# A dense SwiGLU stage with seven-product tiles: lag of the low parts, token sums on another engine, four plain tiles, parts of 5, 5, 6 and 6

## The chip, the cores and the metric

The program runs on one core of a Trainium2 chip. The metric is the device time of one execution in microseconds. Engines are PE (TensorE), DVE (VectorE), ACT (ScalarE), POOL (GpSimd) and SP (SyncE, which here issues most of the loads).

## What is computed

Two layers of a hybrid backbone act on 640 tokens (128 context tokens and 512 latent tokens) of width 1024. The change touches one stage, the dense channel mixer of layer 0, with D_FF = 2816:

```python
def swiglu(u, w_gate, w_up, w_down):
    return (jax.nn.silu(u @ w_gate) * (u @ w_up)) @ w_down
...
    h = rms_norm(x, g_pre2) * (1 + scale2) + shift2
    x = x + gate2 * rms_norm(ffn(h), g_post2)
```

## The kernel before, in words

**Operands in two parts.** Every float32 operand of a product is kept as a high part (a rounded copy in fp32r, made by ACT) and a low part (the rest, made by DVE as operand minus high part). One product is three matmuls: high by high, high by low, low by high. `block_high` (L2766) and `block_low` (L2769) convert a weight block of 128 x 512; `high` (L2757) and `low` (L2761) convert a whole piece of 128 x 1024.

**Tiles.** `stage_dense` walks over 22 feature tiles f of 128 columns of D_FF. The first `PLAIN_F` tiles are plain: gate and up are one piece each, and `features` (L3039) issues 8 k-blocks x 3 x 2 token halves = 48 matmuls of 320 columns per piece, 96 for a tile. The other tiles are combined tiles: a Strassen-like scheme computes gate and up together with seven products (`PRODUCTS`: gate_top, t1, t2, gate_bottom, t3, up_bottom, t4), each 4 x 3 = 12 matmuls of 320 columns (`product`, L3051), 84 for a tile. The four weights t1 to t4 are differences of raw weight blocks (`combine`, L3157, on DVE), each of which is then split like any other block. t1 is up_top minus gate_top, t2 is up_bottom minus t1, t3 is up_bottom minus up_top, t4 is gate_bottom minus t2; t1 and t2 overwrite gate_top's raw block, so each can be formed only when the one before it has been read. The scheme also wants token sums s1 to s4 of the four quarters of the activations (128 x 1280 each), formed once at the stage's start: s1, s2 and s4 on POOL (7 operations, L2881 to L2889), s3 on DVE (3 operations, L3248 to L3250).

**What follows a product.** ACT copies three partial results out of PSUM (`keep_p1` L2925 after gate_top, `keep_p5` L2931 after t1, `keep_u2` L2936 after t2). DVE adds three more to them (`mix_gate` L3203 after gate_bottom, `mix_second` L3209 after t3, `mix_first` L3215 after up_bottom). ACT applies Silu (L2942, and L2947 after t4), DVE multiplies (L3221), ACT takes the high part of the hidden tile (`hidden_high`, L2952), DVE the low part (`hidden_low`, L3227). PE waits for keep_p1 before t2, for keep_u2 before t3, and for mix_gate and mix_second before t4.

**Order.** All queues are written out by hand. On each engine a loop over the entries e (an entry is a weight block in the order in which PE uses it) does what follows the product just finished, and then `make(e + 6)`: ACT the high part and DVE the low part of the block six entries on. The ring holds 8 blocks, so ACT may convert a block when PE has finished the entry seven back. DVE's make waits for ACT's high part of the same block; it also forms the next difference:

```python
                dve.wait_ge(w.hi_done, e + 1)
                w.block_low(dve, e)
                if kind == "gate_top":
                    dve.wait_ge(*w.arrival(entry_of("up_bottom", f)))
                    dve.wait_ge(w.lo_done, e + 1)
                    combine(f, "t1")
```

**Parts.** The tiles come in `DENSE_PARTS`. After each part but the last, PE multiplies the part's hidden tiles by w_down in two column halves (L3089; per tile 2 x 5 token blocks x 3 matmuls of 512 columns = 30), and DVE adds the sums to an accumulator (`keep_sums`, L3237 and L3239). In the last part (L3127) token block b is the outer loop, with 6 matmuls per tile and block, so 30 per tile as well. After block b its residual chain runs on DVE and ACT: add L3292, gate L3297, square and root L3002 and L3004, residual L3306, norm L467, L469, L486 and L494, and PE turns the block (`norm.turn`, L504, 8 small matmuls) after the matmuls of block b + 1. The gate rows that L3297 needs come by a DMA (`ex_rows`) that ACT issues near the end. The next stage begins with L593.

**Loads.** SP loads the raw pieces into four rooms. A room is loaded again when the low part of its last reader is done.

Of the kernel before, what the change touches and what calls it, by code (L numbers as in the profile page):

```python
# [13 lines left out]
F32 = mybir.dt.float32  # L14
# [2627 lines left out]
DENSE_PARTS = (6, 6, 6, 4)  # L2642
DENSE_DEEP = max(DENSE_PARTS)
PLAIN_F = 3
# [6 lines left out]
class DenseWeights:  # L2651
# [10 lines left out]
    RAW_AT = 22816  # L2662
    HI_AT = 28960
    HL_AT = HI_AT + 4 * RING * BLOCK
    LO_AT = HL_AT + 4 * DENSE_DEEP * T + 128
# [5 lines left out]
    def __init__(self, p, l, side, at):  # L2671
# [4 lines left out]
        self.wl = p.placed(f"ex_w_lo{l}", [P, self.RING, BLOCK], F32R, at + self.LO_AT)  # L2676
        sem = lambda name: p.ctx.enter_context(p.nc.semaphore(f"{name}{l}"))
# [54 lines left out]
    def raw_of(self, f, name):  # L2732

        gate, up = self.raw(self.piece_of["gate", f, None]), self.raw(self.piece_of["up", f, None])
        top, bottom = slice(0, BLOCK), slice(BLOCK, 2 * BLOCK)
        return {"gate_top": gate[:, top], "t1": gate[:, top], "t2": gate[:, top], "gate_bottom": gate[:, bottom],
                "t3": up[:, top], "up_bottom": up[:, bottom], "t4": gate[:, bottom], "up_top": up[:, top]}[name]

# [26 lines left out]
    def block_high(self, act, e):  # L2765
        act.activation(self.wh[:, e % self.RING], self.source(e), ACT.Copy).then_inc(self.hi_done, 1)  # L2766

    def block_low(self, dve, e):
        dve.tensor_tensor(self.wl[:, e % self.RING], self.source(e), self.wh[:, e % self.RING].bitcast(F32),  # L2769
                          ALU.subtract).then_inc(self.lo_done, 1)  # L2770


def stage_dense(p, l, h, acc, side, w, at, following, last):
# [12 lines left out]
    token_sum, token_difference, token_high, token_low, pool_c = (p.sig(f"dense_{n}") for n in (  # L2786
        "token_sum", "token_difference", "token_high", "token_low", "pool_chain"))
# [9 lines left out]
    rows = p.placed(f"ex_rows{l}", [P, 2 * D], F32, at + w.S1_AT)  # L2797
    gates = rows[:].rearrange("p (q k s) -> p s k q", k=KD, s=2)
    junk_room = p.placed(f"ex_junk{l}", [P, D], F32, at + w.S2_AT)
# [63 lines left out]
    with nc.Block() as block:  # L2863
# [11 lines left out]
        @block.gpsimd  # L2875
        def _(pool):
            link = chained(pool_c)
            pool.wait_ge(*before.low.at(1))
            plain = lambda half: half.bitcast(F32)
            s1, s2, s4 = s1_raw[:], s2_raw[:], s4_raw[:]  # L2880
            link(pool, pool.tensor_tensor(s1, plain(a21[0]), plain(a22[0]), ALU.add))  # L2881
            link(pool, pool.tensor_tensor(s1, s1, plain(a21[1]), ALU.add))
            pool.tensor_tensor(s1, s1, plain(a22[1]), ALU.add).then_inc(*token_sum.up())
            pool.wait_ge(*token_sum.at(1))
            link(pool, pool.tensor_tensor(s2, s1, plain(a11[0]), ALU.subtract))
            pool.tensor_tensor(s2, s2, plain(a11[1]), ALU.subtract).then_inc(*token_sum.up())
            pool.wait_ge(*token_sum.at(2))
            link(pool, pool.tensor_tensor(s4, plain(a12[0]), s2, ALU.subtract))
            pool.tensor_tensor(s4, s4, plain(a12[1]), ALU.add).then_inc(*token_sum.up())  # L2889

        @block.scalar
        def _(act):
# [13 lines left out]
            def make(e):  # L2906
# [4 lines left out]
                act.wait_ge(*used.at(e - w.RING + 1))  # L2911
# [10 lines left out]
            def keep_p1(f):  # L2922

                act.wait_ge(*after_product("gate_top", f))
                act.activation(p1, bank("gate_top", f), ACT.Copy).then_inc(*copied.up())  # L2925
# [34 lines left out]
            high(4)  # L2960
            act.dma_start(p.gate_rows, p.gate_out[:, l, 1].rearrange("p k s -> p (k s)")).then_inc(*rows_out.up(16))
            token_half(0, s1_raw, s1_hi)
            silu(0)
            high(5)
            token_half(1, s2_raw, s2_hi)
            make(n_plain)
            silu(1)
            token_half(2, s4_raw, s4_hi)
            for e in range(n_plain + 1, n_plain + ahead_by):
                make(e)  # L2970
            act.wait_ge(*token_difference.at(1))
# [546 lines left out]
```

## Time and profile before

| | us |
|---|---|
| median of 3 runs | 2052.81 (2051.3 to 2054.46) |
| the profiled execution | 2053.18 |
| its span in the trace | 2051.3 |
| dense stage in it | 471.8 to 963.5 |
| busy in the whole span: PE, DVE, ACT, POOL | 1893.8, 1435.8, 1165.0, 123.3 |

PE is busy for 92% of the span. The mean granted TensorE clock is 0.973 of full speed. The groups below come from the dense stage only; times are from the span's start. A PE wait is printed as idle time before the matmul that ended it. Since a matmul of 320 columns takes some 0.31 us and the next starts some 0.15 us after it, idle time is shorter than the distance of two starts minus their usual spacing.

### The profile page before, as it was taken

The page shows a single profiled execution, that of the slowest core. Times are in us where ns is not written, and L with a number is a line of the kernel's source. Part 1 is how long each engine was busy: PE and PEld are TensorE (multiplying, and loading weights), DVE is VectorE, ACT ScalarE, POOL GpSimd, SP SyncE. Part 2 cuts the span into 40 slices and gives each one's busy share as a digit, 9 for nine tenths or more (in the row PEclk, how much of TensorE's full clock was granted, in tenths as well). Part 3 has the DMA queues.
Part 4 walks back from the last instruction along what each step waited for, and adds up shares of the span by engine and source line. Part 5 has one row for each costly group of instructions (what it writes and reads, how often), then busy time and mean ns, then how long its engine had stood idle before and what let it go on. Part 6 is the DMA issues. An engine that isn't in the chain of part 4 may idle for free. (4 is left out here: it accounts for less than half of the span.)

```text
span 2051.3 us, 32037 instructions
## 1 busy us (share of the span) xinstructions
PE 1893.8 (92%) x10916; PEld 1585.0 (77%) x10916; DVE 1435.8 (70%) x2209; ACT 1165.0 (57%) x1981; POOL 123.3 (6%) x71
## 2 busy tenths in 40 slices
PE   5998799898899999997997899888999999999998
PEld 2995575598888888886994665787888888888885
DVE  3825766577747556466917766657888888888888
ACT  4215554544424334246216654546888888888885
POOL 0330000005000000000410000002000000000002
PEclk9999899999999999998999999899999999999999
DMA  6204612302232322221206711139977291918394
GB/s 259 97 27 164 233 54 103 103 1 73 67 89 62 103 62 79 66 83 45 97 27 243 261 66 42 53 136 386 410 297 296 83 348 37 372 52 327 110 320 187
DMA packets 133142, 303.44 MB, mean 148 GB/s; under 512 B 20528, under 2 KB 66480, under 8 KB 129968
## 3 DMA queue, kind: packets, MB, share of 16 engines
q1 hardware_dynamic: 126896, 279.51, 38.0%
q10 hardware_dynamic: 3264, 12.07, 1.5%
q0 software_dynamic: 2880, 10.49, 1.4%
q8 instruction: 66, 1.08, 0.2%
q14 instruction: 36, 0.29, 0.0%
HBM read 360.43 MB, written 28.10 MB: 189 GB/s over the span
## 5 line engine op out<-in xcount | busy, mean ns | idle before, releaser
L2587 DVE TENSOR_TENSOR ex_wl<-ex_raw,ex_wh 128x1024 fp32r<-128x1024 f32 x351 | 419.4, 1221 | 27.3 <-ACT ex_wh L2426 15.1
L2426 ACT ACTIVATE ex_wh<-ex_raw 128x1024 fp32r<-128x1024 f32 x351 | 368.1, 1060 | 73.7 <-PE psum L2506 45.6
L2506 PE MATMUL psum<-ex_wh,ex_he_hi 128*128 128x512 f32 (+1 forms) x624 | 242.8, 389 | 4.5 <-DVE ex_he_lo L2559 3.6
L2506 PE MATMUL psum<-ex_wl,ex_he_hi 128*128 128x512 f32 (+1 forms) x624 | 233.6, 374 | 0.0
L2506 PE MATMUL psum<-ex_wh,ex_he_lo 128*128 128x512 f32 (+1 forms) x624 | 233.1, 374 | 0.0
L2769 DVE TENSOR_TENSOR ex_w_lo<-side,ex_w_hi 128x512 fp32r<-128x512 f32 x146 | 100.5, 689 | 121.7 <-ACT ex_w_hi L2766 121.3
L2766 ACT ACTIVATE ex_w_hi<-side 128x512 fp32r<-128x512 f32 x146 | 89.0, 625 | 120.2 <-PE psum L3089 64.3
L3051 PE MATMUL psum<-norm_out,ex_w_hi 128*128 128x320 f32 x608 | 135.1, 310 | 17.8 <-DVE ex_kept L3209 16.3
L2506 PEld LDWEIGHTS psum<-ex_wh,ex_he_hi 128*128 128x128 f32 x624 | 118.2, 190 | 26.8 <-issue 7.9
L2506 PEld LDWEIGHTS psum<-ex_wh,ex_he_lo 128*128 128x128 f32 x624 | 118.5, 190 | 22.3 <-issue 3.2
L2506 PEld LDWEIGHTS psum<-ex_wl,ex_he_hi 128*128 128x128 f32 x624 | 118.1, 189 | 21.0
L708 PE MATMUL psum<-win_hi,norm_out 128*128 128x256 f32 (+1 forms) x640 | 133.1, 300 | 0.1
L3051 PEld LDWEIGHTS psum<-norm_out,ex_w_hi 128*128 128x128 f32 x608 | 101.3, 188 | 21.8 <-issue 21.6
L708 PEld LDWEIGHTS psum<-win_hi,norm_out 128*128 128x128 f32 x640 | 104.7, 188 | 0.4 <-POOL win_lo L621 0.4
L2525 PE MATMUL psum<-ex_wh,ex_hh 128*128 128x512 f32 x260 | 104.6, 402 | 0.0
L2587 DVE TENSOR_TENSOR ex_wl<-x,ex_wh 128x1024 fp32r<-128x1024 f32 x65 | 77.2, 1221 | 38.3 <-ACT ex_wh L2426 38.3
L2525 PE MATMUL psum<-ex_wl,ex_hh 128*128 128x512 f32 x260 | 101.6, 391 | 0.0
L2525 PE MATMUL psum<-ex_wh,ex_hl 128*128 128x512 f32 x260 | 101.5, 390 | 0.0
L1682 DVE TENSOR_REDUCE at_mx<-psum 128x1 f32<-128x640 f32 (+1 forms) x80 | 57.3, 716 | 59.3 <-PE psum L1513 58.9
L1513 PE MATMUL psum<-mx_qkv_room,at_qT 96*128 96x320 f32 (+3 forms) x320 | 92.6, 413 | 6.5 <-ACT at_items_room L1392 5.0
L708 PE MATMUL psum<-win_lo,norm_out 128*128 128x344 f32 (+1 forms) x320 | 96.2, 301 | 0.0
L3051 PE MATMUL psum<-norm_out,ex_w_lo 128*128 128x320 f32 x304 | 93.7, 308 | 0.0
(506 smaller groups left out, 4524.7 us busy)
## 6 DMA issues: line engine op xcount, KB each, us to landing
ex_raw<-moe_gate_up SPq DMA_DIRECT2D x221, 512.0 KB
ex_raw<-moe_w_down SPq DMA_DIRECT2D x143, 512.0 KB
x<-moe_gate_up SPq DMA_DIRECT2D x64, 512.0 KB
wmod_ssd<-w_mod SPq DMA_DIRECT2D x56, 512.0 KB, 6.1
wmod_at<-w_mod SPq DMA_DIRECT2D x24, 512.0 KB, 4.2
side<-ffn_w_gate SPq DMA_DIRECT2D x22, 512.0 KB, 4.0
mx_qkv_room<-w_in SPq DMA_DIRECT2D x10, 1024.0 KB, 5.0
slots<-at_zeros SPq DMA_DIRECT2D x18, 512.0 KB, 14.1
```

Source lines behind the costliest of these rows:

```text
L708: last = pe.matmul(p.psum[:, bank_of(g), 0:width], mh[:, k, j * P:(j + 1) * P], mw[:, k, :], start=(k == 0 and n == 0), stop=(k == KD - 1 ...
L1513: last = pe.matmul(p.psum[:, 2 * (n % 2) + part, 0:w], qT[0:rows, h, b * P:(b + 1) * P], kT[0:rows, h, lo + part * w:lo + (part + 1) * w], ...
L1682: link(dve, dve.tensor_reduce(m[:, 0:1], p.psum[:, 2 * (n % 2):2 * (n % 2) + 2, 0:w], mybir.AxisListType.XY, ALU.max))
L2426: act.activation(wh[:, i % RING], raw_of(i), ACT.Copy).then_inc(*hi_done.up(1))
L2506: last = pe.matmul(p.psum[:, 2 + g % 2, 0:width], h[:, k], w[:, i % RING, cols], start=(k == 0 and m == 0), stop=(k == KD - 1 and m == 2))
L2525: last = pe.matmul(p.psum[:, half], h[:, f], w[:, i % RING, cols], start=(f == 0 and m == 0), stop=False)
L2587: dve.tensor_tensor(wl[:, i % RING], raw_of(i), wh[:, i % RING].bitcast(F32), ALU.subtract).then_inc(*lo_done.up(1))
L2766: act.activation(self.wh[:, e % self.RING], self.source(e), ACT.Copy).then_inc(self.hi_done, 1)
L2769: dve.tensor_tensor(self.wl[:, e % self.RING], self.source(e), self.wh[:, e % self.RING].bitcast(F32), ALU.subtract).then_inc(self.lo_done, 1)
L3051: last = pe.matmul(bank(name, f), m[:, e % w.RING, cols], x[:, k], start=(fresh and k == 0 and n == 0), stop=(k == HALF_K - 1 and n == 2), ...
```

## The change

- `DENSE_PARTS` goes from (6, 6, 6, 4) to (5, 5, 6, 6), `PLAIN_F` from 3 to 4.
- t1 gets a room of its own (`ex_t1`), so it no longer waits until gate_top's block has been split: `begin(e)` forms it ahead of gate_top's low part, after waiting for the landing of both pieces. t2 then follows gate_top's low part, t3 follows t1's, t4 gate_bottom's as before.
- In the loop DVE makes the low part of block e + 5, while ACT still makes the high part of block e + 6.
- All token sums are formed by DVE (10 operations), none by POOL.
- ACT's `hidden_high` moves one entry later, behind keep_p1.
- The last four blocks of w_down, which no longer fit the ring of 8 with six tiles in the last part, get rooms where s1 and s2 lay (`home`, `free_at`). `rows` and `junk` move to other rooms; ACT issues the DMA of `rows` after the last hidden_low and ahead of the last four high parts.

```diff
-DENSE_PARTS = (6, 6, 6, 4)
+DENSE_PARTS = (5, 5, 6, 6)
-PLAIN_F = 3
+PLAIN_F = 4
...
+    def home(self, e):
+
+        n = e - (len(self.entries) - 4)
+        if n >= 0:
+            return tuple(tile[:, n % 2] for tile in self.late[n // 2])
+        return self.wh[:, e % self.RING], self.wl[:, e % self.RING]
+
+    def free_at(self, e):
+
+        first = len(self.entries) - 2 * DENSE_PARTS[-1]
+        return first if e >= len(self.entries) - 4 else e - self.RING + 1
...
         @block.scalar
...
-                act.wait_ge(*used.at(e - w.RING + 1))
+                act.wait_ge(*used.at(w.free_at(e)))
...
+                if entries[e - 2][0] == "t4":
+                    hidden_high(entries[e - 2][1])
                 make(e + ahead_by)
                 if kind == "t3":
                     silu_first(f)
-                if e and entries[e - 1][0] == "t4":
-                    hidden_high(entries[e - 1][1])
             silu_second(n_f - 1)
-            for e in range(whole[0] + ahead_by, len(entries)):
+            make(whole[0] + ahead_by)
+            hidden_high(n_f - 1)
+            make(whole[0] + ahead_by + 1)
+            act.wait_ge(*rows_out.at(16))
+            act.wait_ge(*hid_ready.at(n_f))
+            act.dma_start(rows[:], ...).then_inc(*rows_in.up(16))
+            for e in range(whole[0] + ahead_by + 2, len(entries)):
                 make(e)
-            hidden_high(n_f - 1)
...
         @block.vector
...
+            def begin(e):
+
+                if e < len(entries) and entries[e][0] == "gate_top":
+                    dve.wait_ge(*w.arrival(e))
+                    dve.wait_ge(*w.arrival(e + 5))
+                    combine(entries[e][1], "t1")
...
                 if kind == "gate_top":
-                    dve.wait_ge(*w.arrival(entry_of("up_bottom", f)))
-                    dve.wait_ge(w.lo_done, e + 1)
-                    combine(f, "t1")
-                if kind == "t1":
                     dve.wait_ge(w.lo_done, e + 1)
                     combine(f, "t2")
-                if kind == "t2":
+                if kind == "t1":
                     combine(f, "t3")
...
-                make(e + ahead_by)
+                make(e + ahead_by - 1)
+                begin(e + ahead_by)
                 if before_kind == "t4":
                     multiply(before_f)
```

DVE's queue in one combined tile of the second part, before, from the low part of the preceding tile's hidden tile (L3227) to mix_first (L3215); `ex_w_lo` rows are low parts, L3157 rows are differences:

```order
L3227 TENSOR_TENSOR ex_hl_4951<-ex_sg_hf_4953,ex_hh_4950 128x640
L2769 TENSOR_TENSOR ex_w_lo_468<-side,ex_w_hi_467 128x512
L3157 TENSOR_TENSOR side<-side 128x512
L2769 TENSOR_TENSOR ex_w_lo_468<-side,ex_w_hi_467 128x512
L3157 TENSOR_TENSOR side<-side 128x512
L3203 TENSOR_TENSOR ex_kept_4952<-psum,ex_kept_4952 128x320
L2769 TENSOR_TENSOR ex_w_lo_468<-side,ex_w_hi_467 128x512
L3157 TENSOR_TENSOR side<-side 128x512
L3209 TENSOR_TENSOR ex_kept_4952<-psum,ex_kept_4952 128x320
L2769 TENSOR_TENSOR ex_w_lo_468<-side,ex_w_hi_467 128x512
L3215 TENSOR_TENSOR ex_kept_4952<-psum,ex_kept_4952 128x320
```

The same place in the change (L2787 is the low part, L3166 the difference, L3233 the multiplication, L3239 the hidden tile's low part, L3215 mix_gate, `ex_t` the new room):

```order
L3233 TENSOR_TENSOR ex_sg_hf_4958<-ex_sg_hf_4958,ex_kept_4957 128x640
L2787 TENSOR_TENSOR ex_w_lo_468<-side,ex_w_hi_467 128x512
L3166 TENSOR_TENSOR ex_t_469<-ex_raw_above_466,side 128x512
L3239 TENSOR_TENSOR ex_hl_4956<-ex_sg_hf_4958,ex_hh_4955 128x640
L2787 TENSOR_TENSOR ex_w_lo_468<-side,ex_w_hi_467 128x512
L3166 TENSOR_TENSOR side<-ex_raw_above_466,ex_t_469 128x512
L2787 TENSOR_TENSOR ex_w_lo_468<-ex_t_469,ex_w_hi_467 128x512
L3166 TENSOR_TENSOR ex_raw_above_466<-ex_raw_above_466 128x512
L3215 TENSOR_TENSOR ex_kept_4957<-psum,ex_kept_4957 128x320
```

Each difference that feeds the next one has moved one block forward: t1 of the next tile now stands ahead of the hidden tile's low part, in its own room, and t2 and t3 stand ahead of mix_gate, where t1 and t2 stood. Between mix_gate and mix_second there is one low part and no difference any more (the rows after those shown are a low part and mix_second).

DVE's queue at the stage's start in the change, from s1's first sum to the low parts of the piece after; the sums were on POOL (L2881 to L2889) but for s3's, which stood first:

```order
L3261 TENSOR_TENSOR ex_s_raw_4967<-norm_out 128x1280
L3262 TENSOR_TENSOR ex_s_raw_4967<-ex_s_raw_4967,norm_out 128x1280
L3263 TENSOR_TENSOR ex_s_raw_4967<-ex_s_raw_4967,norm_out 128x1280
L3265 TENSOR_TENSOR ex_s_raw_4968<-ex_s_raw_4967,norm_out 128x1280
L3266 TENSOR_TENSOR ex_s_raw_4968<-ex_s_raw_4968,norm_out 128x1280
L3268 TENSOR_TENSOR ex_s_raw_4969<-norm_out,ex_s_raw_4968 128x1280
L3269 TENSOR_TENSOR ex_s_raw_4969<-ex_s_raw_4969,norm_out 128x1280
L2778 TENSOR_TENSOR ex_w_lo_468<-side,ex_w_hi_467 128x1024
```

Seven sums now stand ahead of the low part of the fifth piece (`low(4)`), where three stood. Behind it follow the gated product of tile 0, the three sums of s3, and `low(5)`.

## Rows read from the trace of the kernel before

**Rows 1.** Window: width, busy PE, PEld, DVE, ACT, POOL, granted clock, DMA share, GB/s
```profile
912.00:960.00 48.00, 34.58 (x146) 27.46 (x144) 33.94 (x48) 32.03 (x58) 0.00 (x0) 0.86 0.14 48
```

**Rows 2.** Waits of PE, 465 to 975 us: total, times, longest
```profile
PE psum L3051 <- DVE ex_kept L3209: 16.3, 15, 1.6
PE psum L504 <- ACT side L494: 14.0, 3, 6.5
PE psum L3051 <- ACT ex_kept L2925: 5.0, 16, 2.1
PE psum L3039 <- DVE ex_w_lo L2761: 3.1, 1, 3.1
PE psum L3051 <- issue: 1.5, 1, 1.5
```

**Rows 3.** Windows, matmuls of L3039, L3051, L3089, L3127: width, PE, PEld, clock, DMA, GB/s
```profile
482.02:510.30 28.28, 28.28 (x192) 28.00 (x192) 1.00 0.16 46
...
757.59:762.93 5.34, 5.34 (x36) 5.23 (x36) 1.00 0.03 9
...
567.08:608.48 41.40, 41.40 (x180) 33.59 (x180) 1.00 0.24 73
...
937.20:942.90 5.70, 5.70 (x24) 4.40 (x24) 1.00 0.00 0
```

**Rows 4.** Timeline in one combined tile: start, us, engine, operation, [idle <-releaser]
```profile
768.15 0.69 DVE L2769 TENSOR_TENSOR ex_w_lo<-side,ex_w_hi 128x512 fp32r<-128x512 f32 x1 [0.78 <-ACT ex_w_hi L2766]
...
769.36 0.48 DVE L3203 TENSOR_TENSOR ex_kept<-psum,ex_kept 128x320 f32<-128x320 f32 x1
...
770.25 0.31 PE L3051 MATMUL psum<-ex_s_hi,ex_w_lo 128*128 128x320 f32 x1
...
770.48 0.69 DVE L3157 TENSOR_TENSOR side<-side 128x512 f32<-128x512 f32 x1
771.09 0.48 DVE L3209 TENSOR_TENSOR ex_kept<-psum,ex_kept 128x320 f32<-128x320 f32 x1
...
771.72 0.38 PE L3051 MATMUL psum<-norm_out,ex_w_hi 128*128 128x320 f32 x1 [1.16 <-DVE ex_kept L3209]
```

**Rows 5.** Groups by line, 465 to 975 us: busy, mean ns, idle before
```profile
L2769 DVE TENSOR_TENSOR ex_w_lo<-side,ex_w_hi 128x512 fp32r<-128x512 f32 x146 | 100.5, 689 | 121.7 <-ACT ex_w_hi L2766 121.3
...
L3157 DVE TENSOR_TENSOR side<-side 128x512 f32<-128x512 f32 x46 | 31.8, 691 | 1.9
...
L3227 DVE TENSOR_TENSOR ex_hl<-ex_sg_hf,ex_hh 128x640 fp32r<-128x640 f32 x19 | 15.6, 820 | 0.8 <-ACT ex_hh L2952 0.8
...
L3203 DVE TENSOR_TENSOR ex_kept<-psum,ex_kept 128x320 f32<-128x320 f32 x19 | 9.2, 486 | 0.3
```

**Rows 6.** Timeline at the stage's start: DVE, POOL and PE
```profile
486.30 4.14 POOL L2881 TENSOR_TENSOR ex_s_raw<-norm_out 128x1280 f32<-128x1280 f32 x1 [88.36 <-DVE norm_out L536]
...
487.65 4.13 DVE L3249 TENSOR_TENSOR ex_s_raw<-ex_s_raw,norm_out 128x1280 f32<-128x1280 f32 x1
...
513.42 1.48 DVE L3183 TENSOR_TENSOR ex_s_lo<-ex_s_raw,ex_s_hi 128x1280 fp32r<-128x1280 f32 x1
...
513.55 0.64 PE L3039 MATMUL psum<-norm_out,ex_w_hi 128*128 128x320 f32 x1 [3.09 <-DVE ex_w_lo L2761]
```

**Rows 7.** Timeline in the last part, DVE and PE
```profile
936.61 1.23 DVE L3292 TENSOR_TENSOR halves<-psum,halves 128x1024 f32<-128x1024 f32 x1 [2.69 <-PE psum L3127]
...
945.69 1.19 PE L504 MATMUL psum<-ident,side 128*128 128x128 f32 x8 [2.65 <-ACT side L494]
...
953.92 1.22 DVE L3292 TENSOR_TENSOR halves<-psum,halves 128x1024 f32<-128x1024 f32 x1 [1.94 <-PE psum L3127]
...
963.48 0.87 PE L593 MATMUL psum<-norm_out,win_hi 128*128 128x320 f32 x2 [0.27 <-DVE win_lo L3317]
```

**Rows 8.** DMA issues, 490 to 915 us: count, KB, median us to landing
```profile
side<-ffn_w_up SPq DMA_DIRECT2D x9, 512.0 KB, 5.2
...
ex_rows<-gate_rows ACTq DMA_DIRECT2D x1, 1024.0 KB, 4.2
```

More of the change, by code:

```diff
@@ L2676, in __init__ @@
         self.wl = p.placed(f"ex_w_lo{l}", [P, self.RING, BLOCK], F32R, at + self.LO_AT)
+        self.t1 = p.placed(f"ex_t1{l}", [P, BLOCK], F32, at + self.T1_AT)
+        late = [P, 2, BLOCK]
+        self.late = [[p.placed(f"ex_w_late{n}_{j}{l}", late, F32R, at + where + 8 * n * BLOCK) for n in range(2)]
+                     for j, where in enumerate((self.S1_AT, self.S2_AT))]
         sem = lambda name: p.ctx.enter_context(p.nc.semaphore(f"{name}{l}"))
@@ L2873, in _ @@
             following.load(sp, 1)
[L2875 to L2889, printed above, removed]
         @block.scalar
@@ L3087, in _ @@
                             claim([out])
-                        for m, (y, x) in enumerate(((hh, w.wh), (hh, w.wl), (hl, w.wh))):
-                            last = pe.matmul(p.psum[:, out, :], y[:, tile, b * P:(b + 1) * P], x[:, e % w.RING, 0:512],
+                        for m, (y, x) in enumerate(((hh, 0), (hh, 1), (hl, 0))):
+                            last = pe.matmul(p.psum[:, out, :], y[:, tile, b * P:(b + 1) * P], w.home(e)[x],
                                              start=(f == first_of[f] and m == 0), stop=(f == last_of[f] and m == 2))
@@ L3247, in _ @@
             plain = lambda half: half.bitcast(F32)
-            link(dve, dve.tensor_tensor(s3_raw[:], plain(a11[0]), plain(a21[0]), ALU.subtract))
-            link(dve, dve.tensor_tensor(s3_raw[:], s3_raw[:], plain(a11[1]), ALU.add))
-            dve.tensor_tensor(s3_raw[:], s3_raw[:], plain(a21[1]), ALU.subtract).then_inc(*token_difference.up())
+            s1, s2, s3, s4 = s1_raw[:], s2_raw[:], s3_raw[:], s4_raw[:]
+            link(dve, dve.tensor_tensor(s1, plain(a21[0]), plain(a22[0]), ALU.add))
+            link(dve, dve.tensor_tensor(s1, s1, plain(a21[1]), ALU.add))
+            dve.tensor_tensor(s1, s1, plain(a22[1]), ALU.add).then_inc(*token_sum.up())
+            dve.wait_ge(*token_sum.at(1))
+            link(dve, dve.tensor_tensor(s2, s1, plain(a11[0]), ALU.subtract))
+            dve.tensor_tensor(s2, s2, plain(a11[1]), ALU.subtract).then_inc(*token_sum.up())
+            dve.wait_ge(*token_sum.at(2))
+            link(dve, dve.tensor_tensor(s4, plain(a12[0]), s2, ALU.subtract))
+            dve.tensor_tensor(s4, s4, plain(a12[1]), ALU.add).then_inc(*token_sum.up())
             low(4)
             gated(0)
+            link(dve, dve.tensor_tensor(s3, plain(a11[0]), plain(a21[0]), ALU.subtract))
+            link(dve, dve.tensor_tensor(s3, s3, plain(a11[1]), ALU.add))
+            dve.tensor_tensor(s3, s3, plain(a21[1]), ALU.subtract).then_inc(*token_sum.up())
             low(5)
-            dve.wait_ge(*token_sum.at(2))
             token_half(0, s1_raw, s1_lo, s1_hi)
-            make(n_plain)
-            gated(1)
-            make(n_plain + 1)
-            dve.wait_ge(*token_sum.at(3))
-            token_half(1, s2_raw, s2_lo, s2_hi)
-            token_half(2, s4_raw, s4_lo, s4_hi)
-            for e in range(n_plain + 2, n_plain + ahead_by):
+            gated(1)
+            low(6)
+            token_half(1, s2_raw, s2_lo, s2_hi)
+            dve.wait_ge(*token_sum.at(3))
+            token_half(2, s4_raw, s4_lo, s4_hi)
+            low(7)
+            begin(n_plain)
+            make(n_plain)
+            gated(2)
+            for e in range(n_plain + 1, n_plain + ahead_by - 1):
                 make(e)
@@ L3282, in _ @@
                     keep_sums(before_f, before_n)
+            make(whole[0] + ahead_by - 1)
+            multiply(n_f - 1)
+            hidden_low(n_f - 1)
             for e in range(whole[0] + ahead_by, len(entries)):
                 make(e)
-            multiply(n_f - 1)
-            hidden_low(n_f - 1)
             dve.wait_ge(*rows_in.at(16))
```

55 lines of the change are left out of this document (30 added, 25 removed).

## The prediction

> **What bounds the kernel now.** I read the share of busy time first, then PE's waits in the dense stage, then windows over each kind of matmul, then the timeline of one combined tile. PE is the bound: inside an uninterrupted run its matmuls follow each other for the whole window at full clock, 2.4 GHz [rows 3]. So the stage's length is matmuls times spacing, plus what PE waits. The spacings are 28.28/192 = 0.147 us for a plain matmul (a plain tile of 96: 14.14 us), 5.34/36 = 0.148 for a combined tile's (84: 12.46), 41.40/180 = 0.230 for w_down's, and 5.70/24 = 0.2375 in the last part [rows 3].
>
> The waits [rows 2]: 15 on DVE's mix_second (L3209), 16.3 us; 16 on ACT's keep_p1 (L2925), 5.0; one of 1.5 in the first combined tile, put down to issue; one of 3.1 in the plain tiles on a low part; and 14.0 in the last part on the norm chain. Idle time understates a wait. In the tile shown the last matmul before t4 starts at 770.25 and t4 at 771.72 [rows 4]: 1.47 less one spacing of 0.148 is 1.32, where the row says 1.16. I add 0.16 to each.
>
> Why is mix_second late? The two operations ahead of it in DVE's queue are a low part and a difference, and mix_gate before them starts only at 769.36 [rows 4], though its product ended near 767.0 (product t3's 12 matmuls and up_bottom's 12 lie between that and 770.25). DVE was held at 768.15 by ACT's high part (0.78 idle), and over the stage DVE waits 121.7 us for high parts [rows 5]. The waits come from a loop of two engines: low part, difference, high part of the difference, its low part, next difference. Each is cheap, but they stand in order ahead of the mixes.
>
> **The change part by part.**
>
> *Lag and t1's room.* DVE then needs high parts that ACT made an entry earlier, and t1 is formed ahead of gate_top's low part, so t2 and t3 come one block sooner. Can one tile run without a wait? DVE's work per tile is 7 low parts of 0.689, 4 differences of 0.691, 3 mixes of 0.486 and 2 operations of 0.82 [rows 5]: 4.8 + 2.8 + 1.5 + 1.6 = 10.7 us, against PE's 12.46. By hand, with PE's products of 1.78 us from 0 and a result visible 0.25 after its end: multiply 0.75 to 1.6 (after the second Silu), low part of t4 to 2.2, next t1 to 2.8, hidden low part 3.15 to 4.0 (after ACT's high part), low and t2 to 5.3, low and t3 to 6.5, mix_gate when its product is there at 7.4 to 7.9, one low part to 8.5, mix_second when t3 is there at 9.15 to 9.65, low and t4 to 10.95, mix_first to 11.4, two low parts to 12.6 (0.14 in the next tile, free before multiply). PE wants mix_second at 10.7: 1.0 us to spare. keep_p1 now stands ahead of hidden_high on ACT: 2.0 to 2.45, wanted at 3.6. In a part's first tile the 5 evictions (3.1) stand where multiply and hidden_low do not; DVE is level again before mix_gate. So I take all these waits as gone: 16.3 + 5.0 + 1.5 = 22.8, plus 32 x 0.16 = 5.1: **-27.9**. Bounds: nothing gone is 0; the rest, if mix_second stays late by half, -15.
>
> *Token sums.* While POOL forms its sums (4.14 each), DVE's own sum takes 4.13; the same shape after POOL has ended takes 1.48 [rows 6]. Low(4) and low(5) are slowed in the same way, and low(5) makes PE wait 3.09 (3.25 with the start correction) before 513.55. With POOL idle, DVE does 7 sums from 486.1: to 496.6; low(4) 1.2 more: 498. PE reaches that piece after 144 matmuls from 482.02, at 503.2. Then the gated product of tile 0 (behind a Silu with a table load, done near 502.4), three sums 4.5, low(5) 1.2: 508.1, wanted at 510.3. Later pieces have over 4 us to spare. So the wait goes: **-3.25**. The operations cost DVE time that hides behind the plain tiles; if a DVE sum should cost 4.13 even with POOL idle, 7 of them end at 515, low(4) at 516.3, and PE waits 13 once. The row is nearest to 1.48, since POOL has nothing else there.
>
> *Fourth plain tile.* 14.14 instead of 12.46: **+1.7**. It hides nothing itself, but it is why the sums have time.
>
> *Parts.* 18 tiles went through L3089, now 16: 2 x 30 x 0.230 = **-13.8**. The last part gets them: 180 matmuls instead of 120. Before, it lasts 910.3 to 963.5 = 53.2, though its 120 matmuls are 28.5: PE waits for the norm chain at three of five turns [rows 2], and the granted clock is 0.86 there [rows 1]. The chain from the add of block 2 (936.61) to its turn (945.69) takes 9.1 [rows 7]. With six tiles PE gives 36 x 0.2375 = 8.55 per block and 0.8 for a turn: 9.35, so the chain just hides and PE stays at full clock. Sum: five blocks 42.75, three turns 2.4, a stall of 0.3 for a late low part in block 0, and the tail from the last matmul to L593 (963.48, with the last add at 953.92 [rows 7]), 9.75: 55.2, so **+2.0**. The rows' DMA (4.2 to landing [rows 8]) is issued at about 3.3 and lands at 7.5, before block 0 ends at 8.9. Bounds: +0.5; at worst all of the added 60 matmuls show, +14.3.
>
> *hidden_high later, late rooms, raw rooms:* nothing. The first low part wanted of the late rooms is ready some 0.5 us ahead; behind them the blocks' first pass covers the rest. If that cover went, it would be one stall of under 1 us.
>
> Sum: -27.9 - 3.25 + 1.7 - 13.8 + 2.0 = -41.25. Against the profiled execution's 2053.18 that is 2011.9; the median of the runs is 0.4 lower. I say **2012**. Nothing later in the program depends on when this stage ends.
>
> A rule of the Trainium skill gives other spacings. TensorE: Matmul & The Clock Gate, section on the back-to-back issue gap, gives columns/2.4 + 2.5 ns at full clock for an isolated gap: 136 ns at 320 columns and 216 at 512. The rows have 148 and 230. By the page the moved w_down matmuls would save 12.9 and the fourth plain tile cost 1.6, so the sum would be 0.8 less of a gain; the measured spacing decides.
>
> **The rivals.**
>
> *A: DVE stays late.* 10.7 of 12.46 leaves 14% of slack, and my schedule gives mix_second 1.0. If each release costs 0.3 more than I allow, the waits shrink but stay, at 0.5 to 1.0 in 15 tiles: 2012 + 8 to 15 = 2020 to 2027. For it: DVE's hand-overs between engines were what made it late. Against: DVE now takes high parts that are an entry old, and in the last tile of a part before, where no differences are formed, there is no mix_second wait (15 waits in 19 tiles).
>
> *B: the last part pays.* Pitch 9.35 against a chain of 9.1 is close; if each turn comes later than the block, or all 60 matmuls show, it is +14.3 instead of +2.0: 2024.
>
> *C: sums slow on DVE*, or low(4) late: up to 13: 2025.
>
> *D, slower than before: the new wait for landings.* `begin` makes DVE wait, a block ahead of the next tile, for both of its pieces. Behind that wait stand the hidden low part, low parts and all mixes. A room is free at about 2.2 in the tile before last, and begin looks 12.3 later. A landing takes 5.2 [rows 8], so 7 us are spare. If landings took L, 17 tiles would pay L - 12.3 each; from L = 14.7 on that eats the 41 us, and at 16 it is +63: 2075. Against it: no load in the stage is near that. The same page of the skill (its part on the clock gate, engine queue depths) calls ScalarE's and VectorE's queues strict FIFO. No row speaks against it: what would be late behind such a wait is all that follows.
>
> *E: the change does not do what it says:* ACT's high parts for t2 and t4 still end the waits, one entry displaced, and another wait of the same size takes their place: only -3.25 + 1.7 - 13.8 + 2.0 = -13.35 remains: 2040.
>
> **How the numbers follow.** A measurement of this kernel can tell about 0.2%, 4 us, from no change. The forecast, with its small terms free (2006 to 2017): 0.77. A 0.09, B 0.05, C 0.02, E 0.02, D 0.03, and 0.02 that something unseen takes nearly all of it. Faster by over 0.2%: 0.95; within: 0.02; slower: 0.03. The range 2006 to 2021 holds the forecast and the near end of A. Its low end takes in +0.5 in the last part, and a start and transitions that I have priced at nothing gaining 4 us.
>
> **What would show it.** The mix_second wait of PE is gone or under 3 us in total, so is keep_p1's; two combined tiles are 12.5 apart, not 14.1. DVE's idle before low parts shrinks while its busy time stays. Seven sums of about 1.5 stand in a row on DVE at 486, and no wait before the sixth piece. w_down's group is x480, the last part 180 matmuls over some 55 us with a clock near 1. A wait of DVE on a DMA before the first difference would be D; turns still ended by ACT with more than 2 us would be B. A stage longer than 460 us, start to L593, would make the prediction wrong.

## The result, and the profile after

The changed kernel takes **2008.59 us** (median of 4 runs, 2005.64 to 2009.72), the kernel before, in runs beside it, 2053.64 (4 runs, 2051.3 to 2055.59): a ratio of **0.9779**, 95% interval 0.9762 to 0.9796. The forecast was 2012 with 2006 to 2021. The profiled executions are 2005.64 and 2053.18, 47.5 apart. All differences below are between profiled executions, unless a median is named.

The first row of the page of after, the share of each engine (busy us, share of the span, instructions):

```profile
PE 1880.9 (94%) x10928; PEld 1582.5 (79%) x10928; DVE 1422.8 (71%) x2205; ACT 1163.6 (58%) x1971; POOL 97.5 (5%) x64
```

TensorE (PE) is still the bound, and POOL has lost its seven token sums. PE's waits in the dense stage, of after, 465 to 935 us (engine and line, what it waited for: us in total, times, longest):

```profile
PE psum L504 <- ACT side L494: 7.1, 2, 6.5
PE psum L3048 <- PEq L1771: 2.9, 1, 2.9
...
PE psum L3060 <- DVE ex_kept L3221: 0.2, 1, 0.2
```

Against [rows 2] the row of 16.3 us on mix_second is gone (L3221 is its line now, with 0.2 in one wait), and so are the 5.0 on keep_p1, the one of 1.5 put down to issue and the 3.1 on a low part. The norm chain holds two turns of the last part instead of three, 7.1 us instead of 14.0. The 2.9 at PEq is PE's own start of the stage and stands in both kernels.

To compare stages I use one measure: from the first matmul behind the turn near 482 us (where [rows 3] begin) to the output's first matmul (L593). The first 10 us of the stage, ahead of that turn, last 9.5 to 10.5 us in the executions of kernels that have the same code there, and the rest of the program varies by a few us. By this measure the stage lasted 481.46 us before and **435.03** after, 46.4 less. It falls into three stretches:

| stretch, us | before | after | difference |
|---|---|---|---|
| plain tiles, to the first combined product | 39.96 | 49.36 | +9.4 |
| combined tiles and their w_down products | 388.33 | 330.91 | -57.4 |
| last part, to L593 | 53.17 | 54.76 | +1.6 |

Windows over each kind of matmul in after, as in [rows 3] (L3048 plain, L3060 combined, L3098 w_down, L3136 last part; PE and PEld busy with their counts, clock, DMA share, GB/s):

```profile
482.39:531.76 49.37, 49.37 (x336) 49.26 (x336) 1.00 0.17 50
...
627.75:640.00 12.25, 12.25 (x86) 12.23 (x84) 1.00 0.42 129
...
646.00:666.00 20.00, 20.00 (x90) 16.54 (x89) 1.00 0.28 77
...
890.07:898.35 8.28, 8.28 (x36) 6.66 (x36) 1.00 0.00 0
```

The plain tiles are one window of 336 matmuls and 49.37 us without a gap, 0.147 each. In the combined tile busy PE fills the whole window: 12.25 us, where the tiles before came every 14.1. DVE in that tile, which begins at 627.75:

```profile
632.49 0.69 DVE L2787 TENSOR_TENSOR ex_w_lo<-ex_raw_above,ex_w_hi 128x512 fp32r<-128x512 f32 x1 [0.22 <-ACT ex_w_hi L2783]
635.01 0.49 DVE L3215 TENSOR_TENSOR ex_kept<-psum,ex_kept 128x320 f32<-128x320 f32 x1 [1.84 <-PE psum L3060]
...
636.77 0.49 DVE L3221 TENSOR_TENSOR ex_kept<-psum,ex_kept 128x320 f32<-128x320 f32 x1 [0.67 <-PE psum L3060]
637.18 0.68 DVE L2787 TENSOR_TENSOR ex_w_lo<-side,ex_w_hi 128x512 fp32r<-128x512 f32 x1
```

Both mixes are now released by PE: mix_gate starts at 635.01, 7.3 behind the tile's start (I had 7.4), mix_second at 636.77, at 9.0 (9.15), where in [rows 4] both stood behind DVE's own work. DVE has become the one that waits for the products. The groups of DVE by line, 465 to 935 us (count | busy, mean ns | idle before):

```profile
L2787 DVE TENSOR_TENSOR ex_w_lo<-side,ex_w_hi 128x512 fp32r<-128x512 f32 x121 | 81.8, 685 | 27.6 <-ACT ex_w_hi L2783 27.6
...
L3166 DVE TENSOR_TENSOR ex_t<-side 128x512 f32<-128x512 f32 x10 | 6.9, 688 | 2.1 <-DMA side<-ffn_w_up 2.1
```

The low part costs what it did, 685 ns against 689 [rows 5], and the idle time before it fell from 121.7 us to 27.6 (in the groups of the other rooms, from 13.9 to 7.9). The second row is the wait that rival D was about: a difference waits twice for a landing, 2.1 us in all, and PE has no wait that answers to it.

DVE at the start of the stage, where [rows 6] had 4.13 us for one sum:

```profile
494.13 1.49 DVE L3268 TENSOR_TENSOR ex_s_raw<-norm_out,ex_s_raw 128x1280 f32<-128x1280 f32 x1
...
497.07 1.22 DVE L2778 TENSOR_TENSOR ex_w_lo<-side,ex_w_hi 128x1024 fp32r<-128x1024 f32 x1
...
507.16 1.22 DVE L2778 TENSOR_TENSOR ex_w_lo<-side,ex_w_hi 128x1024 fp32r<-128x1024 f32 x1
```

Each of the ten sums takes 1.48 or 1.49. The fifth piece's low part starts at 497.07 and the sixth's ends at 508.4, 0.3 later than in my schedule. Last, the window of the last part that answers to [rows 1], and under it two of its turns (L504), the last addition (L3318), the last turn and L593, which answer to [rows 7]:

```profile
866.00:914.00 48.00, 41.94 (x199) 33.99 (x197) 35.31 (x50) 33.49 (x61) 0.00 (x0) 1.00 0.14 47
```

```profile
880.19 1.06 PE L504 MATMUL psum<-ident,side 128*128 128x128 f32 x8 [0.61 <-ACT side L494]
...
898.56 0.85 PE L504 MATMUL psum<-ident,side 128*128 128x128 f32 x6
...
907.87 1.22 DVE L3318 TENSOR_TENSOR halves<-psum,halves 128x1024 f32<-128x1024 f32 x1 [1.58 <-PE psum L3136]
...
915.22 1.94 PE L504 MATMUL psum<-ident,side 128*128 128x128 f32 x8 [6.52 <-ACT side L494]
917.42 0.87 PE L593 MATMUL psum<-norm_out,win_hi 128*128 128x320 f32 x2 [0.27 <-DVE win_lo L3343]
```

The clock is 1.00 in this window, not 0.86. Two blocks apart, the turns start at 880.19 with 0.61 idle and at 898.56 with no idle time printed, 9.2 us a block. Only the last turn waits for the chain in earnest, 6.52, and from the last addition to L593 it is 9.55 us (9.56 in [rows 7]).

### The profile page after: what moved, and what is told of

Its sections match the earlier page's. It is cut to its first block and busy times, and to the rows that moved or that the text cites. A ratio compares the mean times of both kernels' runs of the same rounds, so it can differ in the third digit from the quotient of the medians.

```text
span 2003.9 us, 32045 instructions
## 1 busy us (share of the span) xinstructions
PE 1880.9 (94%) x10928; PEld 1582.5 (79%) x10928; DVE 1422.8 (71%) x2205; ACT 1163.6 (58%) x1971; POOL 97.5 (5%) x64
## 5 line engine op out<-in xcount | busy, mean ns | idle before, releaser
L2426 ACT ACTIVATE ex_wh<-ex_raw 128x1024 fp32r<-128x1024 f32 x351 | 368.0, 1060 | 72.5 <-PE psum L2506 46.4
L3060 PE MATMUL psum<-norm_out,ex_w_hi 128*128 128x320 f32 x576 | 127.3, 308 | 0.2 <-DVE ex_kept L3221 0.2
L2783 ACT ACTIVATE ex_w_hi<-side 128x512 fp32r<-128x512 f32 x121 | 73.8, 625 | 74.4 <-PE psum L3098 53.3
L2787 DVE TENSOR_TENSOR ex_w_lo<-side,ex_w_hi 128x512 fp32r<-128x512 f32 x121 | 81.8, 685 | 27.6 <-ACT ex_w_hi L2783 27.6
L3060 PEld LDWEIGHTS psum<-norm_out,ex_w_hi 128*128 128x128 f32 x576 | 96.3, 187 | 0.7 <-issue 0.4
L1885 PE MATMUL psum<-op_w_hi,op_y_hi 128*128 128x256 f32 x320 | 91.2, 285 | 2.3 <-ACT mx_qkv_room L1812 2.3
```

What stands on the lines that cost most here:

```text
L1885: last = pe.matmul(out, y[:, b % 2, k, :], w[:, i, k, :], start=(k == 0 and n == 0), stop=(k == KD - 1 and n == 2))
L2426: act.activation(wh[:, i % RING], raw_of(i), ACT.Copy).then_inc(*hi_done.up(1))
L2783: act.activation(self.home(e)[0], self.source(e), ACT.Copy).then_inc(self.hi_done, 1)
L2787: dve.tensor_tensor(low, self.source(e), high.bitcast(F32), ALU.subtract).then_inc(self.lo_done, 1)
L3060: last = pe.matmul(bank(name, f), m[:, e % w.RING, cols], x[:, k], start=(fresh and k == 0 and n == 0), stop=(k == HALF_K - 1 and n == 2), ...
```

## The experiments

The eleven kernels are told in the order of what they settle. Times of one execution are compared by the stage as measured above, since the rest of the program moves by a few us between executions.

**Lag or room.** The change cuts the loop of ACT and DVE at two places: the low parts lag by a block, and t1 has a room of its own. The first kernel adds the lag alone to the kernel before; the second takes it from the changed one.

```diff
 # e6_lag_only, on the kernel before
...
-                make(e + ahead_by)
+                make(e + ahead_by - 1)
                 if before_kind == "t4":
                     multiply(before_f)
...
```

> The kernel before with the lag alone: DVE makes the low part of block e + 5, t1 and t2 still overwrite gate_top's block. Theory L (the lag is enough): mix_second's 16.3 us of waits fall under 3, keep_p1's 5.0 stay or shrink, stage 468 to 474. Rival R (only t1's own room cuts the chain): mix_second's waits stay over 10 us, stage 485 to 492.

```diff
 # e5_no_lag, on the changed kernel
...
-                make(e + ahead_by - 1)
                 begin(e + ahead_by)
+                make(e + ahead_by)
...
```

> The changed kernel, DVE without the lag: it makes the low part of block e + 6 again, behind t1, which keeps its own room. Theory R (the room is enough: the chain low part, difference, high part is cut by it): mix_second waits stay under 3 us in total, stage 445 to 448. Rival L (the lag is what freed DVE): the waits come back at least by half, 10 us or more, stage 455 to 467.

PE's waits in e6_lag_only, 465 to 960 us:

```profile
PE psum L504 <- ACT side L494: 14.5, 3, 6.5
PE psum L3039 <- DVE ex_w_lo L2761: 3.1, 1, 3.1
...
PE psum L3051 <- issue: 2.1, 1, 2.1
PE psum L3051 <- ACT ex_kept L2925: 1.9, 1, 1.9
```

and in e5_no_lag:

```profile
PE psum L504 <- ACT side L494: 6.9, 2, 6.5
...
PE psum L3060 <- DVE ex_kept L3221: 1.2, 1, 1.2
```

The lag alone takes all 15 waits on mix_second away. Its stage is 457.97 us, 23.5 shorter than before; what stays in the combined tiles are one wait on keep_p1 of 1.9 and the one put down to issue, now 2.1, both in the first of them. Without the lag but with t1's room, the one wait on mix_second is 1.2 instead of 0.2, again in the first combined tile, and the stage is 435.89, 0.9 longer. So **the lag is enough by itself, and the changed kernel hardly needs it**: with t1's room in place it is worth about 1 us. That fits a loop that needs both of its links, the high part just made and the room just freed. But the room was tried only together with the rest of the change (hidden_high behind keep_p1, the sums on DVE, four plain tiles); that it would be enough by itself in the kernel before is not shown.

**Who made keep_p1 late.** In the changed kernel hidden_high stands behind keep_p1 on ACT. This kernel puts it back, behind the block's high part and Silu.

```diff
 # e4_hidden_high_back, on the changed kernel
-                if entries[e - 2][0] == "t4":
-                    hidden_high(entries[e - 2][1])
                 make(e + ahead_by)
                 if kind == "t3":
                     silu_first(f)
+                if entries[e - 1][0] == "t4":
+                    hidden_high(entries[e - 1][1])
```

> The changed kernel with hidden_high where it stood before, ahead of keep_p1. Theory M (keep_p1 was late because DVE multiplied late; with the lag it no longer does): no wait on keep_p1, stage within 0.5 of 444.6. Rival K (the place of hidden_high made it late): about 0.35 of wait in 14 or so tiles, stage 449 to 451.

The stage is 435.40, 0.4 longer, and among PE's waits there is none on keep_p1. So the new order is not needed. The rows of ACT in the kernel before say what made keep_p1 late there:

```profile
762.07 0.74 ACT L2952 ACTIVATE ex_hh<-ex_sg_hf 128x640 fp32r<-128x640 f32 x1 [1.50 <-DVE ex_sg_hf L3221]
762.72 0.42 ACT L2925 ACTIVATE ex_kept<-psum 128x320 f32<-128x320 f32 x1
```

hidden_high (L2952) waited 1.50 us for DVE's multiplication, keep_p1 (L2925) stood behind it and ended at 763.14, and PE, which wanted it, started t2 at 763.28 after an idle 0.19. With DVE in time, hidden_high ahead of keep_p1 makes nobody wait; e6 agrees, where 15 of the 16 keep_p1 waits went with the mix_second waits though ACT's order was untouched. Whether the new order alone would have ended them in the kernel before wasn't tried. (The single time, 2002.40, is the lowest measured, but the stage says that this is the rest of the program.)

**Parts.** The changed kernel with the parts of before:

```diff
 # e3_parts_6664, on the changed kernel
-DENSE_PARTS = (5, 5, 6, 6)
+DENSE_PARTS = (6, 6, 6, 4)
```

> The changed kernel with the parts of before, 6, 6, 6 and 4; four plain tiles, lag and room stay. Theory (two tiles' 60 matmuls of w_down cost 13.6 us ahead of the last part, and inside it they hide under the norm chain but for 2): 11 to 13 us longer, about 2020. Rival (the waits on the norm chain had shrunk anyway, parts give nothing): within 3 us.

The stage is 449.24, **14.2 longer**; by medians 2017.3 (4 runs), a ratio of 0.9831 to the kernel before (0.9815 to 0.9848), 8.7 us above the changed kernel's. The middle is 345.25, 14.3 longer, where 60 matmuls of w_down make 13.6. The last part is 54.62 against 54.76: in these two kernels it lasts the same with 120 matmuls and with 180. (The medians lie nearer because the sessions differ: against e7 below, timed on the same chip, e3 is 11.0 slower by medians and 12.8 by the stage.) PE's waits in e3:

```profile
PE psum L504 <- ACT side L494: 15.5, 3, 6.5
...
PE psum L3136 <- DVE ex_w_late L2787: 1.6, 1, 1.6
PE psum L3060 <- DVE ex_w_lo L2787: 1.0, 1, 1.0
```

With four tiles PE waits 15.5 us for the norm chain at three turns, with six tiles 7.1 at two. Of the two rows on low parts, the 1.0 lies in a combined tile, which is the 0.7 by which the middle is longer than its matmuls say and some more. The 1.6 lies in the last part's first block, on a low part in the late rooms, and the first addition behind that block waits for the gate rows:

```profile
887.42 1.23 DVE L3318 TENSOR_TENSOR halves<-psum,halves 128x1024 f32<-128x1024 f32 x1 [3.75 <-DMA ex_rows<-gate_rows]
```

So the first turn comes 19.1 us behind the part's first matmul, where it came at 17.1 in the kernel before, whose four tiles took 53.17. I had expected the stage 11 to 13 longer, with a last part about 2 shorter for four tiles. That saving is about what these two delays at the part's start take back; a kernel with four tiles and without them wasn't tried.

**Token sums.** s1, s2 and s4 back on POOL, with ACT's order of before so that no piece is held up behind a slow sum:

```diff
 # e8_pool_sums, on the changed kernel
+        @block.gpsimd
+        def _(pool):
+            link(pool, pool.tensor_tensor(s1, plain(a21[0]), plain(a22[0]), ALU.add))
...
         @block.vector
...
-            link(dve, dve.tensor_tensor(s1, plain(a21[0]), plain(a22[0]), ALU.add))
...
             link(dve, dve.tensor_tensor(s3, plain(a11[0]), plain(a21[0]), ALU.subtract))
```

> The changed kernel with s1, s2 and s4 formed by POOL again. Theory (POOL's operations slow DVE's to about 4 us each, so a low part comes late): the operations of both at 4 us, a wait of 3 us before the sixth piece as in the kernel before, stage 447 to 449. Rival (with four plain tiles there is time for it): no wait, stage 444.6.

The stage is 440.10, **5.1 longer**, and the plain tiles are 54.32 instead of 49.36. Timeline of e8_pool_sums, a stretch each of DVE, POOL and PE:

```profile
488.52 4.17 DVE L3279 TENSOR_TENSOR ex_s_raw<-ex_s_raw,norm_out 128x1280 f32<-128x1280 f32 x1
...
503.11 0.82 DVE L3221 TENSOR_TENSOR ex_sg_hf<-psum,ex_sg_hf 128x640 f32<-128x640 f32 x1 [2.34 <-ACT ex_sg_hf L2915]
503.97 3.02 DVE L3224 CAST ex_hh<-ex_sg_hf 128x640 fp32r<-128x640 f32 x1
...
487.17 4.17 POOL L2898 TENSOR_TENSOR ex_s_raw<-norm_out 128x1280 f32<-128x1280 f32 x1 [89.55 <-DVE norm_out L536]
491.41 4.10 POOL L2899 TENSOR_TENSOR ex_s_raw<-ex_s_raw,norm_out 128x1280 f32<-128x1280 f32 x1
...
503.68 2.96 POOL L2903 TENSOR_TENSOR ex_s_raw<-ex_s_raw,norm_out 128x1280 f32<-128x1280 f32 x1
...
514.44 0.85 PE L3065 MATMUL psum<-norm_out,ex_w_hi 128*128 128x320 f32 x4 [3.08 <-DVE ex_w_lo L2778]
```

The wait of 3.1 us on the low part is back at the same piece. How DVE is slowed can be read from the ends: POOL's first operation ends at 491.34 and DVE's (488.52 + 4.17) at 492.69, 1.35 later, close to the 1.49 that it takes alone; POOL's second begins at 491.41 and ends at 495.51, 2.8 after DVE's end. The two take turns, and each row's length holds the other's work. The operation with one input in PSUM (L3221) takes 0.82, as ever, and the POOL operation that began beside it, ahead of the cast (503.68), takes 2.96, not 4.1. But the cast of 128x640, 0.49 in the changed kernel, takes 3.02. The Trainium skill, SBUF — State Buffer, section "Who interferes with whom", says this of the port pair that the two engines share: a VectorE operation with both inputs in SBUF, or a copy or cast in a two-port mode, and a GpSimd operation that reads SBUF lock each other out for a whole instruction, while one SBUF input outside such a mode doesn't contend. The rows agree, if the cast was in such a mode, which no row shows.

The wait costs more than its row. The same one in the kernel before, windows of PE around it:

```profile
510.00:513.50 3.50, 0.46 (x4) 0.93 0.00 0
513.50:517.00 3.50, 3.44 (x15) 0.58 0.53 151
517.00:522.00 5.00, 5.00 (x37) 1.00 0.01 3
```

After 3.1 us without work the granted clock is 0.58 in the next 3.5 us, with 15 matmuls where 24 fit: some 1.3 us lost behind a wait of 3.1.

**Three plain tiles.** With the sums on DVE, is the fourth plain tile needed? PLAIN_F is 3 again, and the start's order is that of three tiles:

```diff
 # e7_plain3, on the changed kernel
-PLAIN_F = 4
+PLAIN_F = 3
...
+            begin(n_plain)
+            make(n_plain)
             gated(1)
-            low(6)
+            make(n_plain + 1)
             token_half(1, s2_raw, s2_lo, s2_hi)
             dve.wait_ge(*token_sum.at(3))
             token_half(2, s4_raw, s4_lo, s4_hi)
-            low(7)
-            begin(n_plain)
-            make(n_plain)
-            gated(2)
...
-            gated(3)
+            gated(2)
```

> The changed kernel with three plain tiles, start reordered so that the first combined blocks stand where the fourth plain tile's pieces stood. Theory (DVE has formed the sums in time even so, and the fourth plain tile only costs its 12 matmuls): 1.8 us shorter, no wait in the first combined tile, stage 442.8. Rival (the fourth plain tile pays for the sums' time): waits of 2 to 6 us in the first combined tile, stage 445 to 449.

The stage is 436.47, 1.4 longer: the plain tiles are 35.28 (14.1 less), the middle 346.55 (15.6 more, where a combined tile has 12.3). By medians 2006.29 (4 runs, 2005.36 to 2009.09; 0.9785 of the kernel before, 0.9768 to 0.9801), which can't be told from 2008.59. So the stage is not 1.8 shorter, as the theory that I had expected says. The 3.3 us that the middle has too many all lie in the first combined tile, and begin with one wait of PE there:

```profile
523.74 0.69 DVE L3161 TENSOR_TENSOR ex_t<-side 128x512 f32<-128x512 f32 x1
...
524.54 0.63 ACT L2783 ACTIVATE ex_w_hi<-ex_t 128x512 fp32r<-128x512 f32 x1 [2.77 <-DVE ex_t L3161]
...
525.08 0.42 ACT L2938 ACTIVATE ex_kept<-psum 128x320 f32<-128x320 f32 x1
...
525.60 0.53 PE L3055 MATMUL psum<-norm_out,ex_w_hi 128*128 128x320 f32 x2 [2.02 <-DVE ex_w_lo L2787]
```

The printed releaser, a low part on DVE (L2787) of 0.69 us that began at 524.34, had ended at 525.03, 0.57 ahead of PE, where a release took 0.15 in [rows 4]. What ends at 525.50, 0.10 ahead of PE, is ACT's L2938, keep_u2: it stood behind the high part of the next t1 (524.54), which had waited 2.77 us for DVE's difference (L3161, 523.74), and that stood behind the gated product of the third plain tile. DVE has a backlog of one tile's work when the combined tiles begin. The clock accounts for what is left of the 3.3:

```profile
526.00:530.00 4.00, 4.00 (x19) 0.60 0.14 55
530.00:540.00 10.00, 10.00 (x70) 0.99 0.33 104
```

In the 4 us behind the wait 19 matmuls start where 27 fit, at a clock of 0.60: 1.2 us, and with the 2.0 of the wait and the slow interval behind it the 3.3 are told. The fourth plain tile costs 1.8 us of PE and gives DVE the time; **it pays for itself and no more**. Whether three plain tiles win if some of DVE's work at the start goes elsewhere wasn't tried.

**The w_down spacing.** The sum was off by 1.4 us where I expected nothing: w_down's matmuls are 0.227 us apart in after, 0.230 before. Two theories: P, where the rooms of the weight blocks lie in SBUF; Q, what ACT and DVE do meanwhile. In before the ring of high parts begins at an address 32 bytes beyond a multiple of 256 and the ring of low parts 160 beyond one, in after both at a multiple of 1024 (all counted from the stage's base). The first kernel gives the kernel before the rooms of after, the others shift the rooms of after.

```diff
 # e1_before_rooms, on the kernel before
-    RAW_AT = 22816
-    HI_AT = 28960
+    RAW_AT = KEPT_AT + 4 * 2 * D
+    HI_AT = RAW_AT + 4 * D
...
-    LO_AT = HL_AT + 4 * DENSE_DEEP * T + 128
+    LO_AT = HL_AT + 4 * DENSE_DEEP * T + 4 * BLOCK
 # e2_after_shift, on the changed kernel; e9, e10, e11 with 256, 64 and 32
-    HI_AT = RAW_AT + 4 * D
+    HI_AT = RAW_AT + 4 * D + 288
```

> The kernel before with nothing changed but the addresses of its rooms, which are now those of the changed kernel. Stage is from the first L3039 matmul to L593's, 491.7 before and 444.6 in the change. Theory P (where the rooms lie sets the spacing of PE's matmuls): w_down's 512-column spacing falls from 230 to 227 ns, the last part's from 236 to about 230, the waits stay, stage about 489. Rival Q (the spacing fell because the order of the work on ACT and DVE changed): 230 stays, stage 491.7.

> The changed kernel with all rooms from the ring's high parts on shifted by 288 bytes, which is the offset that they had before from a multiple of 1024. Theory P: w_down's spacing goes from 227 back to 229 to 230 ns, stage 444.6 + 2 = 447. Rival Q: 227 stays, stage 444.6.

> The changed kernel with the same rooms shifted by 256 bytes instead of 288. If an address's remainder within 256 (or less) sets the spacing, w_down's stays at 227 ns, stage 443 to 446. If any other place changes the pattern: 229 to 236.

> The same with a shift of 64 bytes. If the remainder within 64 sets the spacing, 227 ns; if that within 128 or 256, 229 to 236.

> The same with a shift of 32 bytes, the remainder that the shift of 288 leaves within 64, 128 and 256. If that remainder sets the spacing: 233 ns as with 288, in the last part too, stage 447 to 449. If it doesn't: 227.

Windows over one part's w_down matmuls, from the first start to the last, so that a window holds the count less one intervals (180 in before and e1, 150 in the others). Before:

```profile
690.83:732.00 41.17, 41.17 (x179) 33.60 (x180) 1.00 0.24 72
```

After:

```profile
640.09:673.91 33.82, 33.82 (x149) 27.98 (x150) 1.00 0.28 78
```

e1_before_rooms:

```profile
688.72:729.34 40.62, 40.62 (x179) 33.60 (x180) 1.00 0.25 73
```

e10_shift64:

```profile
634.15:668.28 34.13, 34.13 (x149) 27.98 (x150) 1.00 0.27 77
```

e11_shift32:

```profile
643.25:678.00 34.75, 34.75 (x149) 27.96 (x150) 1.00 0.27 76
```

| rooms | w_down, ns | stage, us | time, us | kernel before beside it |
|---|---|---|---|---|
| before | 230.0 | 481.46 | 2053.18 | |
| e1: before with after's rooms | 226.9 | 479.19 | 2044.87 | 2049.03 |
| after | 227.0 | 435.03 | 2005.64 | 2053.64 |
| e9: + 256 bytes | 227.0 | 434.92 | 2011.33 | 2063.34 |
| e10: + 64 | 229.0 | 435.88 | 2012.87 | 2063.34 |
| e11: + 32 | 233.3 | 438.10 | 2015.34 | 2063.34 |
| e2: + 288 | 233.3 | 438.19 | 2008.29 | 2049.03 |

**P holds, Q falls.** The kernel before gets after's spacing from the rooms alone, and the changed one loses 3.1 us by a shift of 32 bytes. 288 acts as 32 and 256 as 0, so what counts is the remainder of the address by 256 or by less; since 64 isn't as 0, it is by more than 64. I had expected 229 to 230 for the shift of 288, as in before, and it is 233.3: in before the two rings don't have the same remainder by 256, so the high parts' place isn't all that counts. In before 30 of w_down's matmuls take 6.90 us, 230 ns each, both where DVE is busy for 1.4 us of them (697.73 to 704.63) and where it is busy for 5.7 (711.53 to 718.43), so its work doesn't slow them. The matmuls of 320 columns don't mind: the plain stretch is 49.36 or 49.37 us in after, e2, e9, e10 and e11, and the middle of e11 is 2.8 longer, no more than the 3.0 of its 480 matmuls of w_down. But the columns aren't the only difference: w_down streams its columns out of the shifted rings, while the other products load their weights from them and stream activations. Which room it is (high parts, low parts or the hidden tile's low part, which all move with this edit) wasn't tried.

## Why the prediction was right, step by step

The sum was -41.25 us in the stage; the measured difference is -46.4. Every term has the right sign, and the main mechanisms, DVE late in its loop, the sums slowed by POOL and w_down moved under the norm chain, are confirmed. Three terms were sized too small, the place of the rooms was put at nothing, and one reason that I gave, for keep_p1, isn't needed.

| term | predicted | measured |
|---|---|---|
| waits in combined tiles | -27.9 | -29.9 |
| wait behind the token sums | -3.25 | -4.7 |
| fourth plain tile | +1.7 | +1.8 |
| parts | -13.8 | -15.2 |
| last part | +2.0 | +1.6 |

- **Lag and t1's room, -27.9.** Measured: before, the middle's 388.33 less 540 x 0.230 for w_down and 19 tiles x 84 x 0.1466 leaves 30.2; after, 330.91 less 480 x 0.227 and 18 x 84 x 0.1466 leaves 0.3. The schedule held to within 0.15 us at both mixes. What failed is a size: the step "I add 0.16 to each", which leaves out what a wait costs behind its end. PE right behind the wait of [rows 4]:

```profile
772.08 0.31 PE L3051 MATMUL psum<-norm_out,ex_w_lo 128*128 128x320 f32 x1
772.23 0.46 PE L3051 MATMUL psum<-norm_out,ex_w_hi 128*128 128x320 f32 x2
```

 From 771.72 to 772.08 two intervals take 0.36 us where two at full pace take 0.29 (772.23 shows the pattern). So each of the 32 waits cost its idle time, the 0.16 that I had added, and 0.07 or 0.08 more in the interval behind, some 2.4 us in all. The same slow interval stands in "5.34/36 = 0.148", whose window begins with the end of a wait; at full pace the spacing is 0.147. I credited the two edits together; e6 shows that the lag alone would have done, and e5 that the rest of the change does it without the lag but for 1 us.
- **keep_p1 ahead of hidden_high.** I gave this order as the reason why keep_p1 comes in time. e4 shows that it isn't needed and e6 that 15 of the 16 waits go without it, with DVE's multiplication in time.
- **Token sums, -3.25.** The wait went, as e8 shows from the other side. The missing 1.4 is the clock behind it, which I hadn't priced: of the plain tiles' 39.96 us 240 x 0.1469 = 35.26 is matmuls, and 4.7 the wait with its half clock. The choice of 1.48 for a sum on DVE was right: 1.49.
- **Fourth plain tile, +1.7.** 96 x 0.1469 - 84 x 0.1466 = 1.8. The sentence "it is why the sums have time" holds more exactly for all of DVE's backlog than for the sums (e7).
- **Parts, -13.8.** 60 x 0.230 are the 13.8, and the 480 that remain are 3 ns faster each, 1.4: -15.2. That a new place of the rooms can change PE's pace was not in "late rooms, raw rooms: nothing", the step that failed.
- **Last part, +2.0.** It came at +1.6 for the reason given, a chain about as long as six tiles' block: a pitch of 9.2 (9.35), full clock until the tail, two turns held instead of three. That it is so close is in part luck, since two errors offset each other: a block of 36 matmuls is 8.28, not 8.55, and the turns with their waits are longer than the 0.8 each that I had (the one at 880.19 has 0.61 idle before it). Of the worst case of +14.3, nothing.
- **The rivals.** A (DVE stays late) would have shown 0.5 to 1 us in 15 tiles; there is one wait of 0.2. B would have shown turns behind ACT with over 2 us before the last one; those shown have 0.61 or none. The stage stayed well under the 460 us that I had named as the mark of an error. C fell with sums of 1.49. E fell with the waits themselves: none of their size took their place. D's wait exists, 2.1 us in two places, and is covered; there the "7 us are spare" did not hold. Both lie in stretches of w_down (near 554.6 and 649.1), not in the run of combined tiles that I had counted with. That it would hurt with slower landings wasn't tried.

The terms sum to -46.4. The profiled execution is 47.5 shorter because its first 10 us of the stage and the rest of the program were about 1 us quicker; the medians, 45.05 apart, lie on the other side. So the forecast missed the median by 3.4 us and the stage by 5; that the median is the nearer is chance.

No kernel tried is shown to beat the changed one: e7 is equal to it within the interval, and e4's lower time doesn't come from the stage.

## What to carry to other kernels

When one engine is late for another in every tile, look for the loop that holds it, not for the cheapest operation to remove: here cutting one link (a high part used in the entry in which it is made) ended 15 waits, without any operation less, and with the other link (a room that must be free first) cut as well as the rest of the change made, the first was hardly needed. A wait costs more than the idle time printed for it, by a restart (0.24 us here) and, behind some of the long ones, by the clock, so take spacings from stretches without a wait and add these. Moving work from a filled engine to a stage's end is free only up to the length of the chain that already bounds that end: compare the two lengths before moving more.

## What was not expected of the hardware

- The byte offset of the matmul operands' rooms sets the spacing: w_down's 512-column matmuls come at 227.0 ns with rooms at a multiple of 256 bytes, 229.0 at 64 beyond, 233.3 at 32 or 288 beyond. The Trainium skill, TensorE: Matmul & The Clock Gate, section "Back-to-back issue gap", gives 131 ns as sustained and 216 as isolated at 512 columns; the best stretch here has 227, and the measurement decides.
- Behind a wait the first interval of PE is 0.22 us instead of 0.147, in all 32 waits of the combined tiles before, 16 of them released by ACT and 15 by DVE.
- Behind a wait of 3.1 us the granted clock was 0.58 for 3.5 us, behind one of 2.0 (e7, at 525.60) 0.60 for 4 us and behind one of 2.1 (e6, at 532.44) 0.53 for 3.6 us. But behind the one of 2.1 in the kernel before (at 527.76) it was 1.00 (528 to 531), and 60 us of its combined tiles with waits of up to 1.2 (640 to 700) have 1.00. So the length of a wait alone doesn't tell whether the clock falls to its lower level.
- A cast with one input, 0.49 us alone, took 3.02 beside one of POOL's sums, and an operation with one PSUM and one SBUF input beside the same sums its usual 0.82.
- The releaser printed for a wait on several semaphores can be a third engine's: in e7 it was DVE, and the time of the wait's end fits only ACT's keep_u2.
